# One query tile of the experts kept for both token tiles, and six row buffers in place of eight in the first gather stage

## The reference, cut to what matters

```python
def peer_ffn(h, w_q, sub_keys, u, v):
    q = (h @ w_q).reshape(b, s, PEER_HEADS, 2, PEER_QDIM // 2)      # 1024 -> 2048
    scores = jnp.einsum('bshic,ikc->bshik', q, sub_keys)
    top_s, top_i = lax.top_k(scores, PEER_TOPK)                    # 16 of 128 keys, twice
    ...                                                            # 16 of their 256 sums
    act = jax.nn.gelu(jnp.einsum('td,thkd->thk', xt, u[et]), approximate=False)
    return jnp.einsum('thk,thkd->td', act * gt, v[et])
```

## Time and profile before

| | |
|---|---|
| median of 3 runs | 3012.54 us (3011.54 to 3019.33) |
| profiled execution | 3013.64 us |
| its span | 3011.8 us |
| busy, share of the span | PE 82%, DVE 47%, ACT 29%, POOL 24% |
| DMA, whole span | 1103.07 MB, mean 366 GB/s |
| gathers | 512 of 1 MB, 536.90 MB, 43.2% of the DMA engines' time |
| chain that ended last | PE 41%, DMA 41%, DVE 10%, issue 4%, ACT 4%, POOL 1% |

### The profile page before, as it was taken

How to read it: one execution, slowest core, us unless ns; L and a number is a source line. 1 busy time by engine, 2 the same in 40 slices (tenths; PEclk the granted TensorE clock), 3 DMA queues, 4 the chain that set the end, 5 groups by cost and what they waited for, 6 DMA issues and landing times.

```text
span 3011.8 us, 33582 instructions
## 1 busy us (share of the span) xinstructions
PE 2476.3 (82%) x11878; PEld 1345.0 (45%) x11878; DVE 1426.4 (47%) x3388; ACT 875.9 (29%) x2346; POOL 708.4 (24%) x626
## 2 busy tenths in 40 slices
PE   9999856667999966666799898898897978977777
PEld 8777311112978421212475445464363643632222
DVE  3363100002355201000348886687766787676674
ACT  0231100000022100000225554357334673344333
POOL 4020000001311000000014553334444244344442
PEclk9999887868999987878999999999999999999999
DMA  6337999999434899999929999999999999999997
GB/s 270 133 135 307 414 429 428 428 428 421 175 123 159 367 428 427 428 428 428 375 101 406 419 420 422 421 420 401 410 422 422 422 381 423 421 419 421 421 421 326
DMA packets 123511, 1103.07 MB, mean 366 GB/s; under 512 B 13744, under 2 KB 19280, under 8 KB 23760
## 3 DMA queue, kind: packets, MB, share of 16 engines
q1 hardware_dynamic: 47888, 560.88, 44.7%
q0 software_dynamic: 73728, 536.90, 43.2%
q10 hardware_dynamic: 1728, 3.14, 0.3%
HBM read 1096.68 MB, written 4.19 MB: 366 GB/s over the span
## 4 chain that ended last, share of the span: by engine, by line
PE 41%; DMA 41%; DVE 10%; issue 4%; ACT 4%; POOL 1%; SPq 0%; DVEq 0%; ACTq 0%; POOLq 0%
PE ps L771 17%; DMA wbuf<-in_puv,ar 17%; PE ps L1605 9%; DMA wbuf<-in_w_expert_up 8%; DMA wbuf<-in_w_expert_down 8%; PE ps L962 4%; PE ps L1142 4%; DMA wbuf<-in_w_expert_gate 3%; DVE wbuf L2460 3%; DMA wbuf<-in_w_mem_kv 2%; ACT ar L2524 2%; PE ps L927 2%; PE ps L775 2%; DMA Y<-in_mem 1%; ACT L2524 1%
## 5 line engine op out<-in xcount | busy, mean ns | idle before, releaser
L1605 PE MATMUL ps<-wbuf,ar 128*128 128x512 f32 x1960 | 921.3, 610 | 187.6 <-ACT ar L2524 187.3
L2460 DVE CUSTOM_DVE_ANT_0 wbuf<-wbuf,Y 128x1024 f32<-128x1024 f32 x490 | 601.2, 1227 | 345.9 <-DMA wbuf<-in_puv,ar 332.2
L3162 POOL DMA_INDIRECT wbuf<-in_puv,ar x490 | 551.8, 1126 | 804.0 <-PE ps L1605 712.8
L1142 PE MATMUL ps<-wbuf,ar 128*32 128x512 f32 x2944 | 460.3, 763 | 283.0 <-DMA wbuf<-in_w_expert_down 107.8
L1605 PEld LDWEIGHTS ps<-wbuf,ar 128*128 128x128 f32 x1960 | 355.6, 192 | 678.9 <-issue 677.2
L2524 ACT ACTIVATE ar<-ar 128x1 f32<-128x1 f32 (+1 forms) x1051 | 269.5, 256 | 655.3 <-DVE ar L2460 634.5
L771 PE MATMUL ps<-HT,wbuf 128*128 128x128 f32 (+1 forms) x2640 | 411.4, 313 | 7.2 <-DMA wbuf<-in_w_mem_kv 5.9
L771 PEld LDWEIGHTS ps<-HT,wbuf 128*128 128x128 f32 x2640 | 373.5, 193 | 57.5 <-issue 23.5
L1142 PEld LDWEIGHTS ps<-wbuf,ar 128*32 128x32 f32 x2944 | 93.4, 125 | 633.4 <-issue 211.6
L2521 ACT COPY ar<-ps 128x512 f32<-128x512 f32 (+4 forms) x166 | 76.3, 460 | 707.1 <-PE ps L1142 306.2
L3121 POOL TENSOR_TENSOR sm<-sm,co 128x1 f32<-128x1 f32 x18 | 10.5, 583 | 1109.8 <-DVE sm L1641 1109.6
(11 more groups left out here) (208 smaller groups left out, 2080.4 us busy)
## 6 DMA issues: line engine op xcount, KB each, us to landing
wbuf<-in_w_expert_down SPq DMA_DIRECT2D x64, 2048.0 KB, 32.1
wbuf<-in_w_expert_up SPq DMA_DIRECT2D x62, 2048.0 KB, 30.7
wbuf<-in_w_expert_gate SPq DMA_DIRECT2D x58, 2048.0 KB, 29.9
wbuf<-in_w_in SPq DMA_DIRECT2D x20, 2048.0 KB, 9.2
wbuf<-in_peer_w_q SPq DMA_DIRECT2D x14, 2048.0 KB
wbuf<-in_b_w_in SPq DMA_DIRECT2D x6, 2048.0 KB
wbuf<-in_w_o SPq DMA_DIRECT2D x5, 2048.0 KB, 27.8
wbuf<-in_w_branch_b SPq DMA_DIRECT2D x4, 2048.0 KB, 7.4
```

Of the source, the lines that this page charges most:

```text
L1142: m = T.e.matmul(ps(jobs[n])[32 * k:32 * k + 32, :], lhs(c, k), v[:, 512 * n:512 * n + 512], start=(c == 0), stop=(c == 7), tile_position= ...
L1605: m = T.e.matmul(acc[n][:, :], DG[:, j % 4, :], rows_of(name)[:, 1024 + 512 * n:1536 + 512 * n], start=(j == 0), stop=(j == 127))
L2460: V.did(V.e.tensor_tensor_reduce(u, u, Y[:, i, :], 1.0, 0.0, ALU.mult, ALU.add, DT[:, i, j:j + 1]), f"dot{l}{i}.{j}")
L3162: G.land(G.e.indirect_dma_start(out=rows_of(name), out_offset=None, in_=I["puv"], in_offset=bass.IndirectOffsetOnAxis(ap=IX[:, i, j:j + 1] ...
```

## The change

Query tile 1 is kept in its tile of `wbuf` for both token tiles, as tiles 0 and 3 were. Tiles 2 and 3 are loaded one after the other into the tile of `ma.ukv`, whose two rows leave POOL's order for stage (0,0): six row buffers are left until gather 90, and six after it. The second load of tile 1 is gone; the second load of tile 2 goes into the tile of tile 0 and waits for that. At the first gather of stage (0,1) rows 4 and 5 come in, held by query tile 3.

```diff
@@ sync_program
             query_tile("p0.wq1", 1)
+            tiles.keep(shape["p0.wq1"][0])
+            tiles.release_first(shape["ma.ukv"][0])
             S.wait_ge(*at["ma1.rl7"])
...
             tiles.release_ahead(shape["p0.wq0"][0], 1)
-            query_tile("p0.wq1b", 1)
             query_tile("p0.wq2b", 2)
+            tiles.keep(shape["p0.wq3"][0])
+            tiles.release_first(shape["p0.wq1"][0])
             S.wait_ge(*at["p0.y1"])
@@ other_half (PE)
-                        query_chunk("p0.wq1", 1, 0, n)
+                        query_chunk("p0.wq1", 1, 0, n, False)
...
-                        query_chunk("p0.wq1b", 1, 1, n - 53)
+                        query_chunk("p0.wq1", 1, 1, n - 53)
@@ pool_program
-            rows.order = [0, 1, 2, 3, 10, 4, 5, 11]
+            rows.order = [0, 1, 2, 3, 10, 11]
...
+                    if (l, i, j) == (0, 1, 0):
+                        for k in (4, 5):
+                            rows.held[k] = "p0.wq3"
+                        rows.release_first(4, 5)
```

## The result

The changed kernel takes 3024.8 us (median of 11 runs, 3021.38 to 3030.16), the kernel before 3013.8 us (11 runs, 3011.54 to 3019.33). The ratio is 1.0031, with an interval of 1.0024 to 1.0039: 9 us slower, between 7 and 12. That lies in the stated range of 3005 to 3026, near its upper end. The likeliest case, +0.6 us, did not happen; rival C did. Its price for a mean stay of 16 us, +10.8, is close to the 9 measured, in part by luck, as shown further down.

The account below looks back on a forecast made before the run. PE and DVE pace the first two thirds of the first gather stage, DMA the last. -4.9 + 1.0 + 0 + 2.5 + 2.0 = +0.6 us gave 3014.2 for the profiled execution, forecast 3013.1 us, range 3005 to 3026.

Parts of the forecast that it names:

- The likeliest case: Whole kernel: the sum of all terms, +0.6 us, from -2 to +6; chance 0.61.
- rival C: First gather stage: buffers stay over 15.0 us because attention work stands between rows; +10.8 at mean 16 us; chance 0.20.
- Part 1: First gather stage, near 1838.62 us: the second load of query tile 1 goes, -4.9 us, bounds 0 and -4.96.
- Part 2: Moved query loads: tile 2 ahead of gathers 6 and 7 costs +1.0 us; the other moves cost 0.
- Part 3: First gather stage: six row buffers in place of eight, +2.5 us up to row 99 and +2.0 in rows 116 to 127.
- the last rows: Rows 116 to 127 of the first gather stage: new DMA idle time put at +2.0 us, bounds 0 and +7.
- The walk: Rows 12 to 99, PE's use times fixed, gather n 0.3 us after row n - 6's use: DMA idle 2.7 us more.
- B: First gather stage: DMA stays without a gap, the saved 4.9 us are kept whole, 3007.6 us; chance 0.15.
- D: Something gives more than the bytes, such as gathers landing more evenly without the load at 1838.62; 3002 at most; chance 0.04.
- The markers: Signs from 1590 to 1840 us meant to separate the cases: DMA share, POOL's gathers in 50 us, DVE's waits for gathers.
- A: The sum of the terms, +0.6 us, from -2 to +6, with DMA share 0.97 to 1.00; chance 0.61.
- The sign of being wrong: Second token tile's dots start moved by more than 6 us, or unchanged later stages giving or taking more than 3.

Follow-up runs that it names:

- e4_late2: Changed kernel, but the load of query tile 2 waits until PE has used tile 1 for the first token tile, as before the change: 3027.31 us.
- e8_burst: Changed kernel, but tile 2's second load, the norm row and the output tile wait for the last use of tile 3: 3025.26 us.
- e3_save8: Kernel before, eight buffers, without the second load of query tile 1; some query columns use the wrong weights: 3011.59 us.
- e6_light: Kernel before with six row buffers in the last gather stage alone: 3016.49 us, ratio 1.0000.
- e9_mid: Kernel before with six row buffers in the second gather stage alone: 3028.5 us, ratio 1.0037.
- e10_ten: Kernel before with ten row buffers from gather 84 of the first stage to its end, next stage's output tile loaded later: 3015.7 us.

## Why the prediction was right in its range and wrong in its sum

**Part 1 held.** -4.9 predicted, -5.4 (-8 to -3) measured with eight buffers. The dots that waited for data where the load went out gave the size.

**Part 2 was too dear, by 1.** The dot of gather 7 came 8.7 us later than before. The first gather was 5.3 us late without the change's doing, and gather 5, which waits for ukv and not for the first one, 2.3; so between 3.4 and 6.4 us are the load's, where 4.2 were worked out. SP issued the load at 1588.70 and POOL gather 5 at 1588.94, so the load stood in front of gather 5 already and not behind it. But taking the cause away gained nothing (e4_late2): 0 for the +1.0, as far as these intervals see. In that run row 7 was in time again, 2.3 us late after a start 1.7 late, and row 12 was 8.2 late all the same.

**Part 3 is the step that failed.** Its two terms, +2.5 for the ring and +2.0 for the last rows, are 4.5 us together; six buffers alone cost 15.7 (12 to 19). The walk held PE's use times fixed and asked of each gather whether it could still be in time. It found rows 12 to 99 late by at most 1.3 us and put +2.5 on them; in the trace of six buffers alone the lag grew by 11.3 us from row 12 to row 98, and by 9.1 in the changed kernel. The parts of single executions scatter (6.8 in e8_burst, 13.9 in e4_late2, both with the changed kernel's ring), but in four kernels with eight buffers there (e3_save8, e6_light, e9_mid, e10_ten) the lag changed by 1.2 us or less. The walk began at row 12, so the first twelve rows had no term for the ring: with six buffers gathers 6 and 7 wait for PE's first rows, and 6.0 us were lost there in six buffers alone, 2.4 in the changed kernel. The last rows, from 98 to 127, cost 2.9 in six buffers alone, for +2.0: of the right size.

Why a walk with fixed times falls short is argued, not measured: a gap on the DMA engines makes a row late, a late row moves the work of DVE and ACT behind it and through them PE's next use, and that use is what the gather six rows on waits for. With use times held, each gap stands alone; in the kernel they feed the next. That the lag adds up row by row, and is not a short gap made good, is what the dots show. It was in the text that a late gather frees its own buffer late, and it was then put at 2.5 us without a way to size it.

**Rival C was the mechanism**, with its reason: a ring of six costs 0 us in a stage where PE and DVE have little else, 11 and 16 us in the two stages where they do. Its condition is met in the trace: from the issue of a gather to the end of its matmuls, with the 0.3 us to the next issue, rows 24 to 98 of the changed kernel took 16.5 us on the mean, 13.4 at least. Before, with eight buffers, it was 20.9, because most of a stay is then standing in line. In the last stage six buffers stay 15.4 us and are enough.

**That C's price came out was in part luck.** At its own 12.7 us for each us over 15.0 a stay of 16.5 makes +17. But 75 gathers of rows 24 to 98 took 196.2 us before, 2.62 us each and not 2.50, since other bytes share the stretch; so six buffers give 15.7 us and not 15.0. The 0.8 us above that are some 10 us over 75 rows, and the dots lag 9.0 us more at row 98 than at row 24. The price thus stood on a bound too low and a stay too low, and had no term for the first twelve rows. The range was right because C had been priced into it, not because the sum was.

Its chance, 0.20 against 0.61, looks low in hindsight: PE busy 47.4 and 45.2 of 50 us and DVE 43.3 and 40.5, as the earlier trace rows have it up to 1840, made it likely that a late row finds its engine occupied.

**B** needed a stream without a gap; 402 GB/s for 421 say that there was none such. **D** needed more than the bytes from the saved load; the -5.4 leave room for that only inside their interval.

**The markers** did not all separate. DMA share was to be 0.97 to 1.00 for A and 0.95 or less for C; it was 0.93, 0.99 and 1.01 in the stretches up to 1840 that are shown, 0.98 over all of them. POOL's gathers were to be 19 or fewer in 50 us for C; they were 17, 20 and 19, and the kernel before has 19, 20 and 20 there, so this marker could hardly separate anything. DVE's waits for gathers were to grow beyond 50 us in C; they grew by 3 us, to 32.4, which is what A had. The 22.4 us that they were to grow from left out the far rows' 6.7. Why they stay short isn't shown; DVE, which is late itself, need not wait for what is late with it. The rate in GB/s would have been the marker. The sign of being wrong did speak: the first dot of the second token tile came 12.1 us later, where 6 were the limit. The stages behind it, for which 3 us were allowed, gave back 1.6.

## What to carry to other kernels

A ring of buffers is worth what its last buffer adds under the load of that very stage: the same two buffers cost 16 us beside attention work, 11 beside a state-space mixer, and nothing where PE and DVE had little else to do. So take buffers from the stage with the idlest engines, and count a buffer against its bytes: here 2 MB of ring cost 15.7 us to save a load of 2 MB worth 5. When a ring is cut in a loop, a walk with fixed times gives a lower bound at best; here, with PE 90% and DVE 84% busy from 1590 to 1840 before, it gave 2.5 us for rows 12 to 99 where six buffers alone lost 11. And divide by the pace that the stretch really has, 2.62 us a gather here and not 2.50.

## What had not been expected of the hardware

The DMA share stays near full while the rate falls: 1.01 at 414 GB/s, 0.99 at 399, 0.95 at 367, for 1.01 at 421. The share counts the time that packets take; by these shares and rates a byte takes 8% more of it with five buffers (0.95 / 367) than with eight (1.01 / 421). Why was not tested.

The granted clock is lower in the changed kernel, 0.93 from 1790 to 1890 for 1.00 and 0.97 before. One such place, PE in order of time:

```profile
1825.80 6.68 PE L1608 MATMUL ps<-wbuf,ar 128*128 128x512 f32 x8 [2.85 <-ACT ar L2527]
...
1833.19 3.60 PE L1608 MATMUL ps<-wbuf,ar 128*128 128x512 f32 x8
```

The two rows behind 2.85 us of idle time took 6.68 us, the next two 3.60. The granted clock was 0.50 from 1826 to 1830, the lower of its two levels, 1.2 GHz; it cost PE 3.1 us here. But the clock is not what made the loss. The kernel with six buffers in the second stage still has eight in the first, and there it met the same mean clock as the changed kernel, 0.97 (that run first, then the changed kernel):

```profile
1590.00:1840.00 250.00, 229.30 (x804) 117.23 (x803) 208.62 (x504) 134.91 (x368) 119.04 (x101) 0.97 1.01 418
```

```profile
1590.00:1840.00 250.00, 219.34 (x745) 108.96 (x744) 204.08 (x500) 132.84 (x360) 112.29 (x97) 0.97 0.98 400
```

With eight buffers it moved 418 GB/s at that clock and was 0.2 us late at the last row of the stage, after a start 1.0 late. Whether a fall of the clock costs more when the ring is short was not separated.
